# Reading the moving columns of the hidden-layer products from the last to the first

## The chip, the cores and the metric

The kernel runs on one NeuronCore of one Trainium2 chip. The metric is the device time of one execution in microseconds (us). All data are 32-bit floats; the matrix products use float32r operands, that is 32-bit words whose content was rounded for a single pass through TensorE.

## The reference

Two transformer blocks over 256 tokens of width 1024. Most of the work around this change is in three feed-forward parts:

```python
def _swiglu(x, w_gate, w_up, w_down):                 # twice, D_FF = 2816
    return (jax.nn.silu(x @ w_gate) * (x @ w_up)) @ w_down

def squared_relu_mlp(xn, w_up, w_down):               # once, D_FF_2 = 4096
    return jnp.square(jax.nn.relu(xn @ w_up)) @ w_down
...
x = _layernorm(ALPHA * x + _swiglu(x, w_gate[i], w_up[i], w_down[i]), ln_ffn_g[i], ln_ffn_b[i])
...
x = x + squared_relu_mlp(rms_norm(x, norm_mlp_g[l]), w_up[l], w_down[l])
```

The rest (multi-scale pooling, a differential attention, a mixer with two attentions and a gated recurrence) isn't touched by the change.

## The kernel before

Every operand of a large product is split in two: a rounded half (`hi`) and the rest (`lo`), and a product is hi·hi + lo·hi + hi·lo. Weights come from memory in units of 128x2048 words (1 MB), which rotate through three slots `raw`, `w_hi`, `w_lo`. For each unit SyncE issues two DMAs, ScalarE writes `w_hi` (`round_unit`, L1137), VectorE writes `w_lo = raw - w_hi` (`rest_unit`, L1149), and TensorE uses both. Semaphores `hi_done`, `lo_done` and `unit_done` tie these together; the order on each engine is written out by hand, and there are 308 / 2 = 154 units.

The activations lie in `x_both`, eight blocks of 512 words per partition: in block k the 256 tokens of `x_hi` and behind them the 256 tokens of `x_lo`. There is a second view of the same memory, `x_far`, that begins `SHIFT = 48` words later. `normed` says which stage fills and reads which: the feed-forward parts use the unshifted `x_both`, the attention, the mixer and the gates of the mixer use the shifted one.

A feed-forward part works in chunks of 256 hidden channels. One chunk of gate, and one of up, is one unit each: two PSUM banks (128 hidden channels each), eight blocks k of the contraction. `project_apart` does such a unit in two passes. In the first, `w_hi` is stationary and all 512 columns of `x_both` move, so that the bank holds in one half the product with `x_hi` and in the other that with `x_lo` (16 matmuls of 512 columns). In the second, `w_lo` is stationary and the 256 columns of `x_hi` move (16 matmuls of 256 columns), added into the first half of the bank. The function `apart` issues both. VectorE then adds the two halves of both banks with one TENSOR_REDUCE (`both_halves`, L1628), after which come the nonlinearity, a rounding into `h_hi` and `h_lo`, and the product with `w_down` (`rows`). There `h` is stationary and 512 columns of `w_hi` or `w_lo` move.

The first chunk of each part is done another way (`first_gate_up`, `in_rows`: `x` is stationary), and the last one too, by `project`: for each k three matmuls of 256 columns, `w_hi` by `x_hi`, `w_hi` by `x_lo`, `w_lo` by `x_hi`. `project` is also what the attention, the mixer and the gates use, there with the shifted view:

```python
for k in range(nk):
    c = slice(j * P, (j + 1) * P)
    last = three(o, whi[:, k, c], wlo[:, k, c], hi[:, k, :], lo[:, k, :], k == 0, k == nk - 1)
```

All matmuls go through the helper `mm`, so that the profile lists them under L506. In a name such as `bank<-x_both,w_lo` the matmul writes the bank; where `w` and `x_both` both stand, the names don't say which moves, but the column count does: 128x512 or 128x256 of `x_both,w_...` are those of `apart` and `project` with `x_both` moving; `w_...,x_both` and `w_...,arena_r` are those with the weights moving. The 128 columns of the stationary operand are loaded by an instruction of their own (LDWEIGHTS, engine PEld), which overlaps the matmul before.

One place in the kernel already reads from the last column to the first: in `v_logits` (L1757) VectorE adds a bias `table[:, slot, BACKWARDS[i]]` from SBUF.

Of the kernel before, what the change touches and what calls it, by code (L numbers as in the profile page):

```python
# [21 lines left out]
P = 128  # L22
SEQ = 256
# [154 lines left out]
def build(nc, t, out):  # L178
    with ExitStack() as ctx:
# [12 lines left out]
        x_both, x_far = (x_cells[:, at:at + KT * 2 * SEQ].rearrange("p (k t) -> p k t", k=KT) for at in (0, SHIFT))  # L192
# [72 lines left out]
        banks8 = ctx.enter_context(nc.psum_tensor("bank", [P, 8, 512], F32))  # L265
# [239 lines left out]
        def mm(*a, **k):  # L505
            return nc.tensor.matmul(*a, skip_group_check=True, **k)  # L506
# [16 lines left out]
        def apart(banks, w, cols, ks, first):  # L523

            for j, b in enumerate(banks):
                for k in ks:
                    last = mm(b[:, 0:cols], w[:, k, j * P:(j + 1) * P], x_both[:, k, 0:cols],
                              start=(first and k == 0), stop=(not first and k == KT - 1))
            return last

        def project_apart(slot, banks, narrow_first=False, between=None):

            turns = [(part(w_hi, slot, KT), 2 * SEQ), (part(w_lo, slot, KT), SEQ)]
            if narrow_first:
                turns.reverse()
            for n, (w, cols) in enumerate(turns):
                if n and between:
                    between()
                last = apart(banks, w, cols, range(KT), n == 0)
            return last  # L540

        def first_apart(eng, unit, rounds, banks):

            whi, wlo = (part(w, unit % SLOTS, KT) for w in (w_hi, w_lo))
            eng.wait_ge(hi_done, 2 * unit + 2)
            for h in range(2):
                eng.wait_ge(x_ready, 4 * rounds + 2 * h + 2)
                apart(banks, whi, 2 * SEQ, range(4 * h, 4 * h + 4), True)
            eng.wait_ge(lo_done, unit + 1)
            return apart(banks, wlo, SEQ, range(KT), False)  # L550
# [982 lines left out]
        V = nc.vector  # L1533
# [91 lines left out]

        def both_halves(o, b):

            return V.tensor_reduce(o, banks8[:, b:b + 2, :].rearrange("p a (h t) -> p a t h", h=2),  # L1628
                                   mybir.AxisListType.X, ALU.add)

        def v_ffn(eng, f):
            u0 = U_FFN[f]

            def gate_total(i, gate_unit):

                eng.wait_ge(unit_done, gate_unit + 1)
                both_halves(gate_sum, 4).then_inc(gate_read, 1)
# [7 lines left out]
            def hidden(i, up_unit, direct=None):  # L1645
                eng.wait_ge(unit_done, up_unit + 1)
                total = direct
                if direct is None:
                    both_halves(up_sum, 6).then_inc(up_read, 1)
                    eng.wait_ge(up_read, i + (f * NCH + 1))  # L1650
                    total = up_sum.rearrange("p a b -> p (a b)")
                eng.wait_ge(silu_done, i + (f * NCH + 1))
                ins = V.scalar_tensor_tensor(ffn_h, ffn_t, 0.5, total, ALU.mult, ALU.mult)
                ins.then_inc(product_done, 1)
                if direct is not None:
                    eng.wait_ge(product_done, i + (f * NCH + 1))
                    eng.sem_inc(up_read, 1)
# [38 lines left out]
        def v_mlp(eng):  # L1696
            def square(i, unit, fresh=False, final=False, b=4):
                eng.wait_ge(unit_done, unit + 1)
                if final:
                    eng.wait_ge(relu_done, 2)  # L1700
                    total, other = bank[4], ffn_e
                else:
                    both_halves(gate_sum, b).then_inc(up2_read, 1)
                    eng.wait_ge(up2_read, i + 1)
                    total = other = gate_sum.rearrange("p a b -> p (a b)")
                if not fresh:
                    eng.wait_ge(m_ready, i)
                V.scalar_tensor_tensor(ffn_h, total, 0.0, other, ALU.max, ALU.mult).then_inc(sq_done, 1)
# [467 lines left out]
```

## Time and profile before

| | |
|---|---|
| time, median of 3 runs | 950.97 us (950.43 to 951.21) |
| span of the profiled execution, first to last instruction | 949.5 us |
| granted TensorE clock over the span | 1.000 of full speed |
| PE busy | 938.3 us, 99% |
| PEld busy | 830.4 us, 87% |
| DVE busy | 668.8 us, 70% |
| ACT busy | 473.1 us, 50% |
| DMA | 185 GB/s on average |

The profiled execution spans 949.5 us between its first and last instruction, 1.5 us less than the median of the runs. A matmul's duration in the profile runs to its modelled end, while the next has already begun, so the time that a matmul costs is the distance from its start to the next one's start. It is read from the start times of merged rows: start of the next row minus start of this one, over the count.

### The profile page before, as it was taken

The page shows a single profiled execution, that of the slowest core. Times are in us where ns is not written, and L with a number is a line of the kernel's source. Part 1 is how long each engine was busy: PE and PEld are TensorE (multiplying, and loading weights), DVE is VectorE, ACT ScalarE, POOL GpSimd, SP SyncE. Part 2 cuts the span into 40 slices and gives each one's busy share as a digit, 9 for nine tenths or more (in the row PEclk, how much of TensorE's full clock was granted, in tenths as well). Part 3 has the DMA queues.
Part 4 walks back from the last instruction along what each step waited for, and adds up shares of the span by engine and source line. Part 5 has one row for each costly group of instructions (what it writes and reads, how often), then busy time and mean ns, then how long its engine had stood idle before and what let it go on. Part 6 is the DMA issues. An engine that isn't in the chain of part 4 may idle for free.

```text
span 949.5 us, 15378 instructions
## 1 busy us (share of the span) xinstructions
PE 938.3 (99%) x5895; PEld 830.4 (87%) x5895; DVE 668.8 (70%) x964; ACT 473.1 (50%) x730; POOL 34.6 (4%) x63
## 2 busy tenths in 40 slices
PE   9999999999999999999999999999999999999997
PEld 7988888888898988888887889899999888888886
DVE  4876767676787886667668587975976676666663
ACT  4544444435666454443445566568664454434432
POOL 2010001000000001000001000000000000000000
PEclk9999999999999999999999999999999999999999
DMA  8686666539533377665653945444665546655531
GB/s 295 202 284 227 199 219 209 204 133 266 147 130 101 117 249 256 213 207 178 206 182 109 265 137 134 136 134 137 219 217 181 193 142 213 203 181 189 208 135 44
DMA packets 141648, 175.67 MB, mean 185 GB/s; under 512 B 7152, under 2 KB 119985, under 8 KB 141598
## 3 DMA queue, kind: packets, MB, share of 16 engines
q1 hardware_dynamic: 138384, 166.55, 54.5%
q0 software_dynamic: 2656, 8.31, 2.5%
q8 instruction: 34, 0.56, 0.2%
q10 hardware_dynamic: 558, 0.12, 0.1%
q14 instruction: 16, 0.13, 0.0%
HBM read 173.88 MB, written 1.09 MB: 184 GB/s over the span
## 4 chain that ended last, share of the span: by engine, by line
PE 93%; DVE 5%; issue 1%; ACT 1%; POOL 0%; DVEq 0%; POOLq 0%
PE bank L506 91%; DVE w_lo L1149 1%; PE bank L844 1%; PE bank L638 1%; DVE x_rows L1573 1%; DVE x_rows L1580 1%; DVE stats L1565 1%; ACT w_hi L1137 0%; DVE x_both L1552 0%; DVE arena L2011 0%; PE bank L650 0%; ACT arena L1310 0%; DVE arena L1824 0%; PE bank L717 0%; DVE vareps L1541 0%
## 5 line engine op out<-in xcount | busy, mean ns | idle before, releaser
L1149 DVE TENSOR_TENSOR w_lo<-raw,w_hi 128x1024 fp32r<-128x1024 f32 x308 | 362.6, 1220 | 87.3 <-ACT w_hi L1137 86.8
L506 PE MATMUL bank<-x_both,w_hi 128*128 128x256 f32 (+2 forms) x2032 | 408.3, 325 | 0.0
L506 PEld LDWEIGHTS bank<-x_both,w_hi 128*128 128x128 f32 (+1 forms) x2032 | 336.7, 188 | 37.0 <-issue 5.5
L1137 ACT ACTIVATE w_hi<-raw 128x1024 fp32r<-128x1024 f32 x308 | 307.9, 1050 | 98.1 <-PE bank L506 93.6
L506 PE MATMUL bank<-x_both,w_lo 128*128 128x256 f32 (+1 forms) x1432 | 272.4, 281 | 0.0
L506 PEld LDWEIGHTS bank<-x_both,w_lo 128*128 128x128 f32 (+1 forms) x1432 | 217.0, 190 | 2.6
L506 PE MATMUL bank<-w_hi,arena_r 128*128 128x512 f32 x672 | 189.6, 391 | 0.2 <-DVE arena_r L1712 0.2
L506 PEld LDWEIGHTS bank<-w_hi,arena_r 128*128 128x128 f32 x672 | 124.6, 188 | 25.6 <-issue 0.8
L506 PE MATMUL bank<-w_lo,arena_r 128*128 128x512 f32 x336 | 106.2, 389 | 0.0
L1628 DVE TENSOR_REDUCE arena<-bank 128x512 f32<-128x1024 f32 x52 | 63.5, 1222 | 47.9 <-PE bank L506 47.9
L506 PE MATMUL bank<-w_hi,x_both 128*128 128x512 f32 (+1 forms) x352 | 75.8, 346 | 0.6 <-ACT w_hi L1137 0.4
L506 PEld LDWEIGHTS bank<-w_lo,arena_r 128*128 128x128 f32 x336 | 63.1, 188 | 13.2
L506 PEld LDWEIGHTS bank<-w_hi,x_both 128*128 128x128 f32 x352 | 55.4, 189 | 9.9 <-issue 2.0
L1206 ACT ACTIVATE arena<-arena 128x512 f32<-128x512 f32 x20 | 12.6, 632 | 82.0 <-DVE arena L1628 82.0
L506 PE MATMUL bank<-arena 64*128 64x256 f32 (+7 forms) x346 | 49.1, 351 | 3.2 <-ACT arena L1310 2.2
L1217 ACT ACTIVATE arena_r<-arena 128x512 fp32r<-128x512 f32 x20 | 12.7, 634 | 67.3 <-PE bank L506 61.5
L506 PEld LDWEIGHTS bank<-arena 64*128 64x128 f32 (+2 forms) x346 | 33.7, 186 | 12.6 <-issue 5.9
L506 PE MATMUL bank<-w_lo,x_both 128*128 128x512 f32 (+1 forms) x176 | 41.2, 342 | 0.0
L1310 ACT ACTIVATE arena<-bank 128x512 f32<-128x512 f32 x22 | 13.1, 597 | 49.4 <-PE bank L506 49.4
L1661 DVE TENSOR_TENSOR arena_r<-arena,arena_r 128x512 fp32r<-128x512 f32 x20 | 13.8, 691 | 28.8 <-ACT arena_r L1217 28.8
L1244 ACT ACTIVATE arena_r<-arena 128x512 fp32r<-128x512 f32 x15 | 9.5, 634 | 48.7 <-PE bank L506 47.9
L506 PE MATMUL bank<-arena_r,w_hi 128*128 128x256 f32 x192 | 32.9, 276 | 0.0
(179 smaller groups left out, 604.3 us busy)
## 6 DMA issues: line engine op xcount, KB each, us to landing
raw<-w_up SPq DMA_DIRECT2D x76, 512.0 KB, 4.5
raw<-w_down SPq DMA_DIRECT2D x76, 512.0 KB, 4.2
raw<-w_in SPq DMA_DIRECT2D x60, 512.0 KB, 4.6
raw<-w_gate SPq DMA_DIRECT2D x44, 512.0 KB, 4.7
raw<-w_qkv SPq DMA_DIRECT2D x24, 512.0 KB, 4.8
raw<-w_o SPq DMA_DIRECT2D x16, 512.0 KB, 4.3
table<-bias_vectors POOLq DMA_DIRECT2D x12, 256.0 KB, 4.8
raw<-w_pa SPq DMA_DIRECT2D x4, 512.0 KB, 4.4
```

Of the source, the lines that this page charges most:

```text
L506: return nc.tensor.matmul(*a, skip_group_check=True, **k)
L638: last = nc.tensor.transpose(b[:, k * P:(k + 1) * P], src[:, i, (4 * h + k) * P:(4 * h + k + 1) * P], ident[:, :])
L844: last = nc.tensor.transpose(bank[6 + m][:, c], prob[:, m, c], ident[:, :])
L1137: nc.scalar.activation(w_hi[slot][:, c], raw[slot][:, c], ACT.Copy).then_inc(hi_done, 1)
L1149: last = nc.vector.tensor_tensor(w_lo[slot][:, c], raw[slot][:, c], w_hi[slot][:, c].bitcast(F32), ALU.subtract)
L1206: nc.scalar.activation(ffn_e.rearrange("p (a b) -> p a b", a=2), gate_sum, ACT.Tanh, scale=0.5).then_inc(tanh_done, 1)
L1217: nc.scalar.activation(h_hi[buf], hidden_rows, ACT.Copy).then_inc(h_rounded, 1)
L1244: nc.scalar.activation(h_hi[buf], hidden_rows, ACT.Copy).then_inc(m_rounded, 1)
L1310: nc.scalar.activation(dst, both, ACT.Copy).then_inc(proj_copied, 1)
L1565: ins = V.bn_stats(stats[:, i, h, :], acc[i][h])
L1628: return V.tensor_reduce(o, banks8[:, b:b + 2, :].rearrange("p a (h t) -> p a t h", h=2), mybir.AxisListType.X, ALU.add)
L1661: V.tensor_tensor(h_lo[buf], ffn_h.rearrange("p (a b) -> p a b", a=2), h_hi[buf].bitcast(F32), ALU.subtract).then_inc(h_ready, 1)
```

## The change

`apart` reads the moving columns from the last to the first (a step of -1 word), for both passes. The bank then holds the columns reversed: `x_lo` reversed in its first half, `x_hi` reversed in its second; so the second pass adds into the second half. `both_halves` reads its tokens backwards from PSUM, and what it writes is in the old order. Nothing else changes: no instruction is added, removed or moved on any engine, no wait and no buffer is different. 52 units are concerned: for each feed-forward part with a gate, the gate chunks 1 to 10 and the up chunks 1 to 9 (19, twice), and in the MLP the up chunks 1 to 14.

```diff
@@ apart @@
                 for k in ks:
-                    last = mm(b[:, 0:cols], w[:, k, j * P:(j + 1) * P], x_both[:, k, 0:cols],
+                    last = mm(b[:, 2 * SEQ - cols:], w[:, k, j * P:(j + 1) * P], x_both[:, k, cols - 1::-1],
                               start=(first and k == 0), stop=(not first and k == KT - 1))
@@ both_halves @@
-            return V.tensor_reduce(o, banks8[:, b:b + 2, :].rearrange("p a (h t) -> p a t h", h=2),
+            return V.tensor_reduce(o, banks8[:, b:b + 2, :].rearrange("p a (h t) -> p a t h", h=2)[:, :, SEQ - 1::-1, :],
                                    mybir.AxisListType.X, ALU.add)
```

## Rows read from the trace of the kernel before

**Rows 1.** The page: busy time of each engine, and the chain that ended last
```profile
PE 938.3 (99%) x5895; PEld 830.4 (87%) x5895; DVE 668.8 (70%) x964; ACT 473.1 (50%) x730; POOL 34.6 (4%) x63
PE 93%; DVE 5%; issue 1%; ACT 1%; POOL 0%; DVEq 0%; POOLq 0%
```
**Rows 2.** Groups by shape, PE and DVE: count | busy us, mean ns | idle before
```profile
L506 PE MATMUL bank<-x_both,w_lo 128*128 128x256 f32 x1424 | 270.1, 281 | 0.0
L506 PE MATMUL bank<-x_both,w_hi 128*128 128x512 f32 x832 | 197.7, 390 | 0.0
L1628 DVE TENSOR_REDUCE arena<-bank 128x512 f32<-128x1024 f32 x52 | 63.5, 1222 | 47.9 <-PE bank L506 47.9
```
**Rows 3.** Timeline of PE, one gate and one up unit: start us, us, count
```profile
119.05 3.79 PE L506 MATMUL bank<-x_both,w_hi 128*128 128x512 f32 x16
122.67 4.00 PE L506 MATMUL bank<-x_both,w_lo 128*128 128x256 f32 x32
126.50 3.82 PE L506 MATMUL bank<-x_both,w_hi 128*128 128x512 f32 x16
130.16 0.61 PE L506 MATMUL bank<-w_hi,arena_r 128*128 128x512 f32 x2
```
**Rows 4.** Timeline of PE and DVE, one MLP chunk
```profile
849.49 3.79 PE L506 MATMUL bank<-x_both,w_hi 128*128 128x512 f32 x16
...
853.12 2.08 PE L506 MATMUL bank<-x_both,w_lo 128*128 128x256 f32 x16
...
855.03 0.63 PE L506 MATMUL bank<-w_hi,arena_r 128*128 128x512 f32 x2
855.23 1.22 DVE L1628 TENSOR_REDUCE arena<-bank 128x512 f32<-128x1024 f32 x1 [1.56 <-PE bank L506]
...
857.10 2.35 DVE L1149 TENSOR_TENSOR w_lo<-raw,w_hi 128x1024 fp32r<-128x1024 f32 x2
...
860.50 0.84 PE L506 MATMUL bank<-x_both,w_hi 128*128 128x512 f32 x3
```
**Rows 5.** Timeline of PE, `project` with the shifted view (27 triples)
```profile
660.24 0.39 PE L506 MATMUL bank<-x_both,w_hi 128*128 128x256 f32 x2
660.46 0.28 PE L506 MATMUL bank<-x_both,w_lo 128*128 128x256 f32 x1
...
669.42 0.39 PE L506 MATMUL bank<-x_both,w_hi 128*128 128x256 f32 x2
```
**Rows 6.** Timeline of PE, `project` unshifted (16 triples) and what follows
```profile
926.54 0.40 PE L506 MATMUL bank<-x_both,w_hi 128*128 128x256 f32 x2
926.77 0.28 PE L506 MATMUL bank<-x_both,w_lo 128*128 128x256 f32 x1
...
932.29 0.40 PE L506 MATMUL bank<-w_hi,arena_r 128*128 128x512 f32 x1
```
**Rows 7.** Loads by tile, ns min/median/max: second pass (start), second pass (middle), first pass
```profile
L506 PEld LDWEIGHTS bank<-x_both,w_lo x2: 188/188/188, 122.4 to 122.7; 128*128 128x128 f32 x2
L506 PEld LDWEIGHTS bank<-x_both,w_lo x26: 192/192/192, 122.9 to 125.9; 128*128 128x128 f32 x26
L506 PEld LDWEIGHTS bank<-x_both,w_hi x15: 187/188/188, 119.0 to 122.2; 128*128 128x128 f32 x15
```
**Rows 8.** Loads by tile, 660.3 to 671 us, `project` with the shifted view
```profile
L506 PEld LDWEIGHTS bank<-x_both,w_hi x64: 187/188/188, 660.1 to 670.8; 128*128 128x128 f32 x64
```
**Rows 9.** Timeline of PE, `project` shifted, a unit of the attention (6 triples)
```profile
255.74 0.40 PE L506 MATMUL bank<-x_both,w_hi 128*128 128x256 f32 x2
...
257.86 0.40 PE L506 MATMUL bank<-x_both,w_hi 128*128 128x256 f32 x2
```
**Rows 10.** Groups by shape, DVE: the backward read of the table
```profile
L1757 DVE CUSTOM_DVE_ANT_0 arena<-bank,table 128x256 f32<-128x256 f32 x24 | 10.1, 420 | 0.0
...
L1757 DVE CUSTOM_DVE_ANT_0 arena<-bank,table 128x128 f32<-128x128 f32 x24 | 6.9, 288 | 5.7 <-PE bank L506 5.0 <-DVE arena L1814 0.7
```
**Rows 11.** Timeline of PE, transposes of 128 plain float32 columns
```profile
763.70 1.03 PE L638 MATMUL bank<-ident,arena 128*128 128x128 f32 x8
764.57 0.61 PE L506 MATMUL bank<-ident 128*128 128x128 f32 x4
```

## Prediction

> **What bounds the kernel.** I read the page first: TensorE is busy 99% of the span and carries 93% of the chain that ended last, with VectorE at 5% [rows 1]. Nothing else needs to be known to say that only a change of the matmuls' own pace, or a stall of TensorE, can move the time. The groups by shape then give the sizes: 832 matmuls of 512 columns in first passes, and 16 for each of 52 units, so 832 again, in second passes (they are part of the 1424 with 256 columns), and 52 reductions of 1222 ns [rows 2].
>
> The pace comes from the timeline. First pass: (122.67 - 119.05) / 16 = 226.3 ns, and in the MLP (853.12 - 849.49) / 16 = 226.9 ns; about 0.443 ns per column, the same in both [rows 3, 4]. Second pass: (126.50 - 122.67) / 32 = 119.7 ns, and in the MLP (855.03 - 853.12) / 16 = 119.4 ns; 0.467 ns per column [rows 3, 4]. All 52 units together: 832 x 226.5 + 832 x 119.6 = 188.4 + 99.5 = 288 us, 30% of the span. The reader should see that the second pass is slower per column than the first, by 119.6 - 226.5 / 2 = 6.4 ns a matmul.
>
> That difference isn't a property of 256-column matmuls. `project` with the shifted view does 81 of them in 669.42 - 660.24 = 9.18 us, 113.3 ns each [rows 5]; the same function unshifted does 48 in 932.29 - 926.54 = 5.75 us, 119.8 ns each [rows 6]. Both keep TensorE full, both read the same words at the same step; only the address of the moving operand differs, by 48 words. So where the moving read begins relative to the stationary one costs 6.5 ns. The loads show the same: 188 ns where the pace is 113.3 [rows 8], 192 ns in the middle of an unshifted second pass, but 188 for its first two, and 188 in the first pass, which is unshifted too [rows 7]. The loss thus appears only when one load follows another every 256 columns, so that a load's last reads fall together with the first reads of the matmul that it serves. A 512-column matmul leaves the load 113 ns of room, and loses nothing. I read this as a collision in SBUF between the end of the stationary read and the start of the moving read; the addresses of the first start at multiples of 128 words, those of the second at multiples of 512.
>
> **The change, part by part.**
>
> *Instructions.* None is added, removed or moved; the cost can only be in the pace of what is there.
>
> *First pass, 832 matmuls.* The amount read is the same. If a step of -1 streams like +1, the cost is 0: the pace stays 226.5 ns, since the load has room. What would the step itself cost? No matmul of the trace reads its moving operand backwards. The nearest row is on another engine: VectorE's sum with the backward table takes 288 ns for 128 columns and 420 ns for 256, so (420 - 288) / 128 = 1.03 ns a column [rows 10]. The forward reduction takes at most 1222 / 1024 = 1.19 ns per element read, its fixed part included [rows 2], so the backward read has no penalty there. Lower bound 0, upper bound by the row in which a TensorE column costs most, the plain float32 transposes: (764.57 - 763.70) / 8 = 109 ns for 128, 0.85 ns a column against 0.443, a factor of 1.9 or about 2 [rows 11]. I take 0, because the only backward row says 0.
>
> The Trainium skill ("Vector Engine (DVE) Microarchitecture Reference", Measured stream behaviour on trn2) says that a VectorE port streams at full rate only in runs of two adjacent words that begin on an 8-byte boundary, and gives 1.30 ns a column for pairs that begin on an odd word against 1.054. A backward read begins on an odd word (511 or 255), so the rule, if it went by the first word read, would speak against the change. By that ratio, 1.23, an estimate from the page, the two passes would cost 832 x 0.23 x (226.5 + 113.3) ns = 65 us more, where the row gives 0. The row of the backward table, which also begins on odd words (127 and 255), doesn't bear that reading of the rule out on VectorE.
>
> *Second pass, 832 matmuls.* The moving read now begins at word 255 of its block instead of word 0, and ends at word 0. If the collision is between the load's end and the matmul's start, it depends on which words these are. Fastest end: the pace of the shifted view, 113.3 ns, a gain of 119.6 - 113.3 = 6.3 ns x 832 = 5.2 us. Between: one unit of the attention runs shifted at (257.86 - 255.74) / 18 = 117.8 ns [rows 9], which would give 1.8 x 832 = 1.5 us. Slow end without a new mechanism: another 6.5 ns, that is 126. I take the fast end. The stationary read ends at one edge of its 128 words; if it ran upwards its end would be an edge 127 against a moving start at 0, and the collision would have to be between different words; if it runs downwards it ends at word 0, where the moving read begins, and both meet. 
>
> *The reduction, 52 times.* It reads 1024 words of PSUM in pairs that lie 256 words apart, and goes through the tokens downwards instead of upwards. No row shows a backward PSUM read; the table row bounds it from below at 0, and twice its length, +1222 ns, is the bound from above. I take 0. In the MLP it is also covered: it ends at 856.45, and TensorE asks for that bank again at 860.50, 4.05 us later; the split of weights that it would delay, 857.10 to 859.45, is for the unit that starts after the next one, at about 866 [rows 4]. So even doubled it would cost nothing; without that cover it would be 52 x 1.22 = 63 us.
>
> *Sum.* 0 - 5.2 + 0 = -5.2 us. On the profiled execution 949.5 becomes 944.3; the runs lie 1.5 us above their span, so 950.97 becomes 945.7. Everything is gained on the path: TensorE is never idle there, its groups show 0.0 us of idle time before them [rows 2], and VectorE at 70% and ScalarE at 50% [rows 1] have room to follow a pace that is 1 to 2% quicker.
>
> **Rivals.**
>
> *No change.* The collision stays: the other edge of the moving block meets the load just as the first did (a load that ends at its word 127 would meet a start at 255, the same place in a period of 128 words), and the second pass remains at 119.6. For it: all block addresses are multiples of 128 words, so the mirrored start is as aligned as the old one. Time 951.0.
>
> *Slower, mildly.* Both reads now run downwards from an aligned edge at the same moment, and the moving read loses the 6.5 ns of a collision twice in 512 columns, also in the first pass, where until now it lost nothing: 832 x 13 ns = 10.8 us with the second pass as it was. Time 961.8. It decides from the moment that a first-pass matmul takes more than 226.5 + 6.3 = 232.8 ns, because then it eats the gain of the second.
>
> *Slower by much.* TensorE takes in a column in 0.443 ns, faster than any row shows for another engine; if it does so by fetching two neighbouring words at once, and does this only upwards, a column costs about twice: 832 x (226.5 + 113.3) = 283 us, less the 5.2 us at most. Time about 1230. For it: the rate in [rows 3] needs some such fetch, and no row shows it downwards on TensorE. Against it: VectorE at full rate downwards [rows 10]. The page's figure for odd words, above, would be a lighter form of the same mechanism, and shares its chance.
>
> **How the numbers follow.** Gain by a freed second pass (945.7, own range 944.8 to 949): 0.43. No change (within 0.2%, which is about what a measurement of this kernel can tell): 0.26. Mildly slower: 0.12. Much slower: 0.19. The likeliest is 945.7. A range from 944.5 to 963 holds the first three, 0.81; the much slower case is left out. A partial gain such as 117.8 ns (949.5) lies at the border and is counted half to each side. So: faster 0.42, same 0.27, slower 0.31.
>
> **What would show it.** In the timeline of the changed kernel, the second pass of a gate and an up unit should take 32 x 113.3 = 3.63 us instead of 3.83, and the loads under it 188 ns instead of 192; the first pass should still be 226.5 ns a matmul; the reduction 1222 ns. If the loads stay at 192, the collision didn't move. If first-pass matmuls are at 233 ns or more, or near 450, one of the two slower rivals is right. I'd be wrong altogether if the step of -1 changes the rate of the stream, since 30% of the span hangs on it.

## The result and the profile after

The changed kernel takes 954.75 us, the median of 5 runs (954.36 to 955.15), beside 950.65 us (950.43 to 951.21) for 5 runs of the kernel before. The ratio is 1.0042, with a 95% interval of 1.0029 to 1.0054: slower by 0.4%, about 4 us. The prediction said 945.7 us and faster. In the table further down, the 949.37 us of `second_back` are the median of 12 runs of which one took 1032.06 us at a granted clock of 0.851; without it, as in the ratio, the median is 949.30 us.

The page of the changed kernel, its span, its busy times and the chain that ended last; these answer to [rows 1]:

```profile
span 953.4 us, 15378 instructions
PE 942.2 (99%) x5895; PEld 829.4 (87%) x5895; DVE 668.6 (70%) x964; ACT 472.9 (50%) x730; POOL 35.1 (4%) x63
PE 93%; DVE 5%; issue 1%; ACT 1%; POOL 0%; DVEq 0%; POOLq 0%
```

The span grew by 953.4 - 949.5 = 3.9 us, and PE's busy time by 942.2 - 938.3 = 3.9 us. The busy time of the loads (PEld) fell by 1.0 us, that of the other engines changed by at most 0.5, the chain reads as before, and the granted clock is 0.999 against 1.000. So no wait has come in and nothing has been reordered: the matmuls themselves take longer. The groups by shape of the changed kernel say which ones; they answer to [rows 2]:

```profile
L506 PE MATMUL bank<-x_both,w_lo 128*128 128x256 f32 x1424 | 269.1, 280 | 0.0
L506 PE MATMUL bank<-x_both,w_hi 128*128 128x512 f32 x832 | 202.8, 398 | 0.0
L1628 DVE TENSOR_REDUCE arena<-bank 128x512 f32<-128x1024 f32 x52 | 63.5, 1221 | 50.9 <-PE bank L506 50.9
```

The 832 matmuls of the first passes went from 390 to 398 ns, the mean of the 256-column group fell by 1 ns, and the backward reduction is unchanged at 1221 ns. The paces stand in the timeline of PE of the changed kernel (start us, us, count), the same gate and up unit as in [rows 3]:

```profile
119.69 3.90 PE L506 MATMUL bank<-x_both,w_hi 128*128 128x512 f32 x16
123.43 3.95 PE L506 MATMUL bank<-x_both,w_lo 128*128 128x256 f32 x32
127.21 3.90 PE L506 MATMUL bank<-x_both,w_hi 128*128 128x512 f32 x16
130.95 0.63 PE L506 MATMUL bank<-w_hi,arena_r 128*128 128x512 f32 x2
```

The 32 matmuls in a row are two second passes: the kernel issues the up unit of a feed-forward part with a gate in the other order, its 256-column pass first (`narrow_first` in `project_apart`), so that the row at 127.21 is the up unit's pass of 512 columns.

First pass: (123.43 - 119.69) / 16 = 233.8 ns a matmul, before 226.3. Second pass: (127.21 - 123.43) / 32 = 118.1 ns, before 119.7. The loads under that second pass, by tile (ns min/median/max), answer to the second line of [rows 7]:

```profile
L506 PEld LDWEIGHTS bank<-x_both,w_lo x31: 187/188/189, 123.4 to 127.0; 128*128 128x128 f32 x31
```

They are back at 188 ns, from 192, and yet the pace is 118.1 and not 113.3 ns. That already speaks against the prediction's reading, in which the long load and the slow pace were one collision.

To see where the whole time went, I added up, for each kind of matmul, the distances from each one's start to the next matmul's start. These sums are worked out from all 5895 start times of each trace; since PE is never long without work, they make up the span but for its ends. In us (worked out before rounding, so that differences can be off by 0.1 from those of the rows):

| kernel | first passes, 832 of 512 columns | `w_lo` by `x_both`, 1432 of 256 | `w_hi` by `x_both`, 1200 of 256 | all other matmuls | time, median | ratio to before, 95% |
|---|---|---|---|---|---|---|
| before | 189.2 | 172.8 | 140.2 | 440.2 | 950.65 | |
| changed | 194.3 | 171.7 | 140.3 | 440.1 | 954.75 | 1.0042 [1.0029, 1.0054] |
| first_back | 194.4 | 173.0 | 140.0 | 439.7 | 956.02 | 1.0052 [1.0039, 1.0065] |
| second_back | 188.8 | 171.9 | 140.6 | 439.4 | 949.37 | 0.9978 [0.9970, 0.9987] |
| second_both | 188.8 | 172.1 | 140.0 | 439.1 | 949.05 | 0.9977 [0.9968, 0.9986] |
| before_shift | 194.1 | 167.9 | 139.5 | 440.0 | 950.98 | 0.9998 [0.9990, 1.0007] |
| after_shift | 194.2 | 171.3 | 139.7 | 440.0 | 954.08 | 1.0031 [1.0019, 1.0043] |
| rest_shift | 189.5 | 171.2 | 140.1 | 439.5 | 949.32 | 0.9981 [0.9972, 0.9990] |
| rest_16 | 189.2 | 171.6 | 140.0 | 439.9 | 948.84 | 0.9976 [0.9966, 0.9987] |
| both_16 | 191.2 | 168.4 | 139.4 | 440.4 | 947.84 | 0.9966 [0.9952, 0.9979] |

For the change: first passes +5.1 us, the `w_lo` matmuls -1.1 us, the rest within 0.1. Together +4.0, the span's 3.9. Each kernel's ratio is against runs of the kernel before on the same chip (medians of 950.65 to 951.23 us). The other rows are the experiments below; their names are used there.

### The profile page after: what moved, and what is told of

The parts are those of the page before. It is cut to its first block, busy times and chain, and to the rows that moved or that the text cites. A ratio compares the mean times of both kernels' runs of the same rounds, so it can differ in the third digit from the quotient of the medians.

```text
span 953.4 us, 15378 instructions
## 1 busy us (share of the span) xinstructions
PE 942.2 (99%) x5895; PEld 829.4 (87%) x5895; DVE 668.6 (70%) x964; ACT 472.9 (50%) x730; POOL 35.1 (4%) x63
## 4 chain that ended last, share of the span: by engine, by line
PE 93%; DVE 5%; issue 1%; ACT 1%; POOL 0%; DVEq 0%; POOLq 0%
PE bank L506 91%; DVE w_lo L1149 1%; PE bank L844 1%; PE bank L638 1%; DVE x_rows L1573 1%; DVE x_rows L1580 1%; DVE stats L1565 1%; ACT w_hi L1137 0%; DVE x_both L1552 0%; DVE arena L2011 0%; PE bank L650 0%; ACT arena L1310 0%; DVE arena L1824 0%; PE bank L717 0%; DVE vareps L1541 0%
## 5 line engine op out<-in xcount | busy, mean ns | idle before, releaser
L506 PE MATMUL bank<-x_both,w_hi 128*128 128x256 f32 (+2 forms) x2032 | 413.5, 328 | 0.0
L1628 DVE TENSOR_REDUCE arena<-bank 128x512 f32<-128x1024 f32 x52 | 63.5, 1221 | 50.9 <-PE bank L506 50.9
```

## The experiments

### The two passes apart

`first_back` turns only the first pass, `second_back` only the second. Of `first_back` the edit in `apart` is this; `second_back` has the two branches the other way round, and both read backwards in the reduction as the change does. Each of them then adds columns of different tokens to one another; the amount of work is that of the change.

```diff
-                    last = mm(b[:, 0:cols], w[:, k, j * P:(j + 1) * P], x_both[:, k, 0:cols],
+                    move = x_both[:, k, cols - 1::-1] if cols == 2 * SEQ else x_both[:, k, 0:cols]
+                    last = mm(b[:, 2 * SEQ - cols:], w[:, k, j * P:(j + 1) * P], move,
```

first_back:

> Only the first pass (512 columns, hi weights) reads backwards; the second pass reads forwards but still adds into the upper half of the bank, so its columns are added in the wrong order (the amount of work is unchanged). If the cost of the change sits in the first pass alone, every one of its 832 matmuls takes 233.3 instead of 226.7 ns: +5.1 to 5.5 us, about 956.0 us. Rival, that the two passes influence each other through the order in which they follow: less than +4 us. Second pass: 119.7 ns, as before, if its gain in the changed kernel came from its own direction; about 118.3 if it came from what precedes it.

second_back:

> Only the second pass (256 columns, lo weights) reads backwards; the first reads forwards into the bank, so the halves are summed in mixed order (wrong sums, same work). Theory that start positions matter: first pass back at 226.7 ns, second pass at about 118.3 ns as in the changed kernel, so about 1.2 us less than before, 949.4 us. Rival, that a step of -1 is what costs: second pass slower than 119.7, time above 951.

The timeline of PE of `first_back`, and then of `second_back`, at the same place in the program:

```profile
119.50 3.90 PE L506 MATMUL bank<-x_both,w_hi 128*128 128x512 f32 x16
123.23 4.00 PE L506 MATMUL bank<-x_both,w_lo 128*128 128x256 f32 x32
127.07 3.90 PE L506 MATMUL bank<-x_both,w_hi 128*128 128x512 f32 x16
```

```profile
118.39 3.79 PE L506 MATMUL bank<-x_both,w_hi 128*128 128x512 f32 x16
122.02 3.95 PE L506 MATMUL bank<-x_both,w_lo 128*128 128x256 f32 x32
125.81 3.79 PE L506 MATMUL bank<-x_both,w_hi 128*128 128x512 f32 x16
```

`first_back`: 233.1 ns in the first pass and (127.07 - 123.23) / 32 = 120.0 in the second. `second_back`: 226.9 and (125.81 - 122.02) / 32 = 118.4. So each pass carries its own share: the backward first pass costs 5.2 us in the sums, the backward second pass gives back 0.9 us, and 0.4 us more comes from first passes that run at 226.9 (in the kernel before they are at 226.3 and at 228.8 in turn, [rows 3]). Another 0.8 us of `second_back`, and 1.1 us of `second_both` below, lies in the other matmuls, which the edits don't touch; the sums are of one execution each, and what made that part isn't shown. The loss is in the first pass, to which the prediction had given a cost of zero.

### Another place for the moving read

If the start address is what counts, the unshifted activations can be moved instead. `before_shift` is the kernel before, with both views at 48; `after_shift` is the changed kernel with the same edit.

```diff
-... for at in (0, SHIFT))
+... for at in (SHIFT, SHIFT))
```

before_shift:

> The kernel before, but all stages use the view that begins 48 words later (forward reading). Theory of a collision at the place where the moving read begins: second pass at 113.3 instead of 119.7 ns, 832 x 6.3 = 5.3 us less, and the unshifted project units gain 144 x 6.5 = 0.9 us: about 944.6 us. Rival, that the 48 words act only where the three products of project alternate: no change, 950.7 us.

after_shift:

> The changed kernel with the same shift by 48 words everywhere. Theory that the backward read is slow only because it begins at the last word of a block, the same place modulo 128 words at which the stationary read begins: first pass back at 226.7 and second at 113.3 ns, about 944.6 us, the same as forwards with the shift. Rival, that the step of -1 itself costs 16 cycles a matmul: first pass stays at 233.3 ns, about 950 us or more.

The timeline of PE of `before_shift`:

```profile
118.53 3.89 PE L506 MATMUL bank<-x_both,w_hi 128*128 128x512 f32 x16
122.26 3.80 PE L506 MATMUL bank<-x_both,w_lo 128*128 128x256 f32 x32
125.90 3.89 PE L506 MATMUL bank<-x_both,w_hi 128*128 128x512 f32 x16
```

Forward, 48 words further, the second pass does run at (125.90 - 122.26) / 32 = 113.8 ns, and the first at 233.1 ns, in nothing but a forward read. The sums say -4.9 us and +4.9 us, and the time is that of before (0.9998), not the 944.6 us expected: the rival's time, but not by the rival's reason, since the second pass did gain. In `after_shift` both stay where the backward read has put them: 233.1 and 117.8 ns, by (122.74 - 119.01) / 16 and (126.51 - 122.74) / 32. So the backward read doesn't answer to the shift, and 512-column matmuls do lose 6.7 ns at an offset that 256-column ones like.

### The matmuls alone

Four kernels hold nothing of the reference but matmuls: float32r words of value one in SBUF, eight blocks of 512 moving columns and of two times 128 stationary ones as in `x_both` and a unit, 16 to 32 matmuls for each configuration (in `micro4` twice a single one), straight after one another. Each of the four was executed once, at a granted clock of 1.00 in all the rows used here. The stationary tensor alternates, so that each configuration is a row of its own in the timeline, and the pace is once more start of the next row minus start of this one, over the count. That average holds the few matmuls in which the pace settles too. Each configuration also has another one just before it; that this matters comes out at the end, in `micro4`.

`micro1` sweeps the direction and the offset of the moving read:

```python
at = k * 512 + shift
a = moving[:, at:at + width]
if back:
    a = moving[:, at:at + width][:, ::-1]
s = src[:, k * 256 + (i // 8 % 2) * P + w_shift:][:, 0:P]
```

> Only matmuls, 24 to a configuration, all of the reference left out: 512 or 256 moving columns, forwards or backwards, the moving operand shifted by 0 to 127 words and then the stationary one by 16, 48 or 64. Theory of places: the pace depends on shift and direction together. 512 forwards 226.7 at all shifts; 512 backwards 233.3 at shift 0 and 226.7 at 48; 256 forwards 120 at 0 and 113.3 at 48; 256 backwards about 118 at 0. Over the shifts each slow case should fill a stretch as wide as one piece of memory that can serve one reader at a time, and come back with a period. Rival, that the step costs by itself: 512 backwards 233.3 at every shift.

The timeline of PE of `micro1`. In this order: 512 forward at offset 0 and (next row) 4; 512 backward at offset 0 and 4; 256 forward at 0 and 4, and at 16, 32 and 48; then 512 forward at offset 0 with the stationary read moved by 16 and (next row) by 48 words.

```profile
20.00 5.60 PE L66 MATMUL bank<-moving,w_even 128*128 128x512 f32 x24
25.44 5.72 PE L66 MATMUL bank<-moving,w_odd 128*128 128x512 f32 x24
...
86.55 5.76 PE L66 MATMUL bank<-moving,w_even 128*128 128x512 f32 x24
92.15 5.76 PE L66 MATMUL bank<-moving,w_odd 128*128 128x512 f32 x24
...
154.00 3.03 PE L66 MATMUL bank<-moving,w_even 128*128 128x256 f32 x24
156.87 3.02 PE L66 MATMUL bank<-moving,w_odd 128*128 128x256 f32 x24
...
162.53 2.89 PE L66 MATMUL bank<-moving,w_odd 128*128 128x256 f32 x24
165.25 3.01 PE L66 MATMUL bank<-moving,w_even 128*128 128x256 f32 x24
168.09 2.89 PE L66 MATMUL bank<-moving,w_odd 128*128 128x256 f32 x24
...
222.10 5.75 PE L66 MATMUL bank<-moving,w_even 128*128 128x512 f32 x24
227.69 5.66 PE L66 MATMUL bank<-moving,w_odd 128*128 128x512 f32 x24
```

512 columns: (25.44 - 20.00) / 24 = 226.7 ns forward, (92.15 - 86.55) / 24 = 233.3 backward. 256 columns at 16: (165.25 - 162.53) / 24 = 113.3 forward. The whole sweep, worked out the same way from unrounded start times, so that a value can differ by some tenths from the rounded rows:

| ns a matmul, by offset in words | 0 | 4 | 8 | 16 | 32 | 48 | 64 | 80 | 96 | 112 | 120 | 127 |
|---|---|---|---|---|---|---|---|---|---|---|---|---|
| 512 forward | 226.7 | 231.5 | 233.5 | 228.9 | 232.1 | 233.3 | 227.5 | 229.6 | 232.8 | 233.5 | 233.2 | 230.3 |
| 512 backward | 233.3 | 233.3 | 233.4 | 233.4 | 236.6 | 233.2 | 233.5 | 233.5 | 233.5 | 233.2 | 233.5 | 239.8 |
| 256 forward | 119.6 | 119.1 | 116.7 | 113.5 | 118.5 | 113.8 | 119.2 | 118.0 | 118.5 | 117.8 | 118.2 | 117.0 |
| 256 backward | 118.1 | 120.0 | 118.0 | 119.9 | 119.8 | 118.0 | 118.3 | 119.7 | 119.8 | 118.0 | 117.7 | 120.3 |

For 512 columns forward, 64 to 112 read like 0 to 48, within 1 ns: a period of 64 words. For 256 columns 64 reads like 0, but 80 and 112 don't read like 16 and 48. With the moving read at 0 and the stationary one moved by 16, 48 or 64 words instead, 512 backward stays at 233.2 to 233.3. But 512 forward doesn't stay at 226.7: it takes 233.0, 229.2 and 227.1 ns, and 256 forward 114.3, 113.3 and 119.9. So the good pace of a forward read hangs on where the stationary read lies as well: moving that one alone by 16 words costs (227.69 - 222.10) / 24 - 226.7 = 6.2 ns, about what the backward read costs.

So a forward read has better and worse offsets, and 226.7 at offset 0 is the best of them for 512 columns; a backward read has no good one among these twelve, nor among the three places of the stationary read. A theory of the start address, mine or the rival's, would have one.

`micro2` takes what would collide away: the same matmuls with 96, 64 and 32 stationary columns, so that the load reads down to a quarter of the words. It also has moving reads with a step of 2.

```python
a = moving[:, at:at + width * step:step]
...
s = src[:, k * 256 + (i // 8 % 2) * P:][:, 0:m]      # m = 128, 96, 64, 32
```

> Only matmuls again, 24 to a configuration, the reference left out: stationary operands of 128, 96, 64 and 32 columns under the same moving reads, then 128 and 384 moving columns, odd starts and steps of 2. Theory that the 16 cycles are a collision of the backward moving read with the stationary read that runs beside it: they shrink with the stationary columns, 512 backwards about 233.3, 231.7, 230.0, 228.3 ns for 128, 96, 64, 32, and don't depend on the moving columns (384 backwards 6.7 ns over 384 forwards). Rival, that a step of -1 costs the moving read itself: 233.3 whatever the stationary operand, and the loss goes with the moving columns (256 backwards half of 512). Third, a fixed cost of starting a backward read: 6.7 ns at every size of both.

512 columns backward at offset 0 took 233.2, 236.4, 233.3 and 233.2 ns with 128, 96, 64 and 32 stationary columns; forward 226.7, 230.2, 230.5 and 231.5. 256 columns forward took 119.2, 116.2, 114.1 and 113.8, and backward 118.3, 119.8, 117.6 and 117.8. The backward 512-column pace doesn't fall with the stationary read. The gap to the forward one does, from 6.5 to 1.7 ns, but because the forward read gets slower, not because the backward one gets faster. Of the 256-column reads the forward one got faster here; `micro3` below has 117.9 ns for that same read over 32 stationary columns, so that isn't a property of the narrow stationary operand alone. Nor is the loss a fixed fee: with 128 stationary columns, over the last twelve matmuls of each row, 384 columns took 173.3 ns forward and 177.8 backward, and 128 columns 111.7 either way. The steps of 2, from the timeline of PE of `micro2` (128 stationary columns with step 2, then step -2; 32 with step 2):

```profile
202.46 5.60 PE L72 MATMUL bank<-moving,w_even 128*128 128x256 f32 x24
207.88 5.78 PE L72 MATMUL bank<-moving,w_odd 128*128 128x256 f32 x24
213.48 5.66 PE L72 MATMUL bank<-moving,w_even 128*32 128x256 f32 x24
```

(207.88 - 202.46) / 24 = 225.8 ns for 256 columns: a step of 2 costs as much as 512 neighbouring words, with step -2 233.3, as much as 512 words backwards. That is what one would see if words came in pairs at least, as the much-slower rival said; but then they come downwards as well, since a step of -1 costs 3%, not 100%.

`micro3` asks how far apart the pieces must be that are read in the wrong order. It reads 512 columns in groups of g words: either the words within each group downwards and the groups upwards ("words"), or the groups downwards and the words within upwards ("groups"). A second sweep changes the width, with 32 stationary columns.

```python
a = a.rearrange("p (a b) -> p a b", b=g)
a = a[:, :, ::-1] if way == "words" else a[:, ::-1, :]
```

> Only matmuls, 32 to a configuration, the reference left out. 512 moving columns of one block, reversed in part: either the words inside groups of 2 to 256 run down while the groups run up, or the groups run down while their words run up. Then 64 to 512 columns, up and down, under a stationary operand of 32 columns. Theory that a backward read pays a fixed part at its start: one step back in a group costs nothing, groups of any size with words downwards stay near 226.7, and down minus up is 4 to 7 ns at every width. Rival, that the cost goes with the words read downwards (through some piece of memory of a certain size): down minus up grows from 1 ns at 64 columns to 6.7 at 512, and the cost changes at one group size.

The timeline of PE of `micro3` (the table below it is from unrounded starts again): up, down; words of 4, groups of 4, words of 8, groups of 8, words of 16, groups of 16; groups of 32, words of 64, groups of 64, words of 128.

```profile
20.55 7.42 PE L68 MATMUL bank<-moving,w_even 128*128 128x512 f32 x32
27.80 7.63 PE L68 MATMUL bank<-moving,w_odd 128*128 128x512 f32 x32
...
50.01 7.43 PE L68 MATMUL bank<-moving,w_even 128*128 128x512 f32 x32
57.28 7.63 PE L68 MATMUL bank<-moving,w_odd 128*128 128x512 f32 x32
64.75 7.62 PE L68 MATMUL bank<-moving,w_even 128*128 128x512 f32 x32
72.21 7.63 PE L68 MATMUL bank<-moving,w_odd 128*128 128x512 f32 x32
79.67 8.70 PE L68 MATMUL bank<-moving,w_even 128*128 128x512 f32 x32
88.20 7.64 PE L68 MATMUL bank<-moving,w_odd 128*128 128x512 f32 x32
...
103.14 7.61 PE L68 MATMUL bank<-moving,w_odd 128*128 128x512 f32 x32
110.59 7.63 PE L68 MATMUL bank<-moving,w_even 128*128 128x512 f32 x32
118.06 7.43 PE L68 MATMUL bank<-moving,w_odd 128*128 128x512 f32 x32
125.33 7.63 PE L68 MATMUL bank<-moving,w_even 128*128 128x512 f32 x32
```

| ns a matmul of 512 columns, by g | 2 | 4 | 8 | 16 | 32 | 64 | 128 | 256 |
|---|---|---|---|---|---|---|---|---|
| words down, groups up | 227.2 | 227.2 | 233.1 | 266.4 | 233.3 | 233.3 | 233.4 | 233.4 |
| groups down, words up | 233.4 | 233.4 | 233.4 | 233.7 | 232.6 | 227.2 | 227.2 | 227.2 |

Up to four words read in the wrong order cost nothing once the pace has settled (226.7 ns over the last twelve; the 227.2 hold two slower matmuls at the start), as long as the fours go upwards, and neither do stretches of 64 or more in the wrong order. Everything else costs 6 to 7 ns, and 16 words turned round cost 40. In these runs the loss follows the order in which pieces of at least 4 words are read inside a stretch of 64 words. It is not a fee for a start or a turn, since a read of 256 turned pairs pays nothing and one of two turned halves of 256 words pays all of it.

The Trainium skill ("Advanced Engine Details and Errata", Memory Cachelines) says that SBUF has lines of 16 bytes, which is 4 words, and that accesses which stay on the same line run at full rate. The free turn of 4 words, 227.2 ns in the table above, agrees with that; that turned stretches of 64 words are free while turned ones of 8 to 32 aren't is not in that rule, nor is the cost of fours read upwards but taken in falling order, 233.4 ns.

The width sweep, up and down: 117.9 and 117.8 ns at 256 columns, 146.3 and 146.7 at 320, 173.4 and 175.6 at 384, 202.2 and 204.5 at 448, 231.3 and 233.2 at 512. Below 384 columns the two directions differ by at most 0.4 ns in this sweep; at 256 columns `micro2` had 113.8 and 117.8 ns for the same two reads, behind other ones.

### The second pass by other means

`second_both` asks whether the gain of the backward second pass needs a backward write. The first pass is forward; the second reads and writes its bank backwards, so every sum is the reference's:

```diff
+                    out_, move = b[:, 0:cols], x_both[:, k, 0:cols]
+                    if cols == SEQ:
+                        out_, move = b[:, cols - 1::-1], x_both[:, k, cols - 1::-1]
...
```

> The kernel before, but the second pass alone reads backwards and also writes its bank backwards, so that the halves stay in order and the sums are right; the reduction reads forwards. If only the moving read's direction counts: second pass at 118.2 ns as in the changed kernel, first at 226.7, about 949.4 us. Rival, that a backward write to PSUM costs: second pass above 119.7, time above 951.

226.9 and (125.68 - 121.90) / 32 = 118.1 ns, 949.05 us: like `second_back`. Writing PSUM backwards costs nothing that shows.

`rest_shift` and `rest_16` keep both reads forward at offset 0 and move the stationary side: `w_lo` of the hidden-layer units lies 48 or 16 words further in a wider tile. The three tiles are wider by 64 words each, so that what is laid out behind them may lie further on too, by a multiple of 64 words.

```diff
+        w_lo_cells = [sb(f"w_lo{s}", [P, UW + 64], F32R) for s in range(SLOTS)]
...
+        w_lo_far = [v[:, SHIFT:SHIFT + UW] for v in w_lo_cells]      # 16 in rest_16
...
-            turns = [(part(w_hi, slot, KT), 2 * SEQ), (part(w_lo, slot, KT), SEQ)]
+            turns = [(part(w_hi, slot, KT), 2 * SEQ), (part(w_lo_far, slot, KT), SEQ)]
```

rest_shift:

> The kernel before, forwards, with w_lo of the gate, up and MLP-up units written and read 48 words further on, so that the second pass has the offset at which 256 columns took 113.3 ns in the first microbenchmark, while the first pass keeps the offset 0 at which 512 columns take 226.7. Theory that the pace is set by the distance of the two read addresses modulo 64 words: second pass 113.3 instead of 119.7, 832 x 6.3 = 5.3 us, and the row products and projects that use this w_lo (128 matmuls) 0.9 us more: about 944.7 us. Rival, that the gain of the second pass is given back in the first, as it was when both were shifted: 950.7 us.

rest_16:

> As the version with w_lo of the hidden units 48 words further on, but 16 words. If the pace is set by the distance of the two addresses modulo 64 words, 16 and 48 are not the same; in the first microbenchmark both gave 113.3 ns at 256 columns. If the second pass reaches 113.3: about 945 us. If it stays at the 117.6 ns at which the 48-word version settled: about 949.3 us.

Second passes at (125.31 - 121.55) / 32 = 117.5 and (126.40 - 122.63) / 32 = 117.8 ns, first passes at 226.9: 949.32 and 948.84 us. The 113.3 ns of the matmuls alone, which `micro1` gave for the stationary shifts of 16 and 48, didn't come, with one exception inside `rest_shift` itself: worked out from single starts, the 33 passes that stand right behind a pass of 512 columns settle at 118 ns, and the 3 that have four transposes in between (`between` in `project_apart`) at 113; in `rest_16` it is 2 of those 3. The same 256-column matmul, at the same offsets, thus has more than one pace, and something else decides. `micro4` asks whether it is the pass before: 16 matmuls of 512 columns, then 32 of 256, at varied offsets; at its end reads up and down in turn.

> Only matmuls, the reference left out, in the order in which the kernel has them: 16 of 512 columns at offset 0 and then 32 of 256 with the stationary or the moving operand at another offset; then matmuls of 512 and of 256 columns read upwards and downwards in turn. Theory that the pace of a pass depends on the state in which the pass before leaves the two reads: 256 columns at offset 48 settle at 117.6 ns behind 512 columns at offset 0, as in the kernel, and at 113.3 behind 512 at offset 48. Rival, that something else of the kernel (other engines' accesses) holds it at 117.6: 113.3 in both. In the mixed passes, if the loss lies in the hand-over from one matmul to the next, up-down and down-up differ from one another; if it lies inside a downward read, the matmul read downwards takes 233.3 and the one read upwards 226.7.

The timeline of PE of `micro4`: 512 at offset 48, 256 at offset 48; 512 at 16, 256 at 16; 512 at 0, 256 at 48, 512 at 0, 256 at 16, and the next row.

```profile
73.06 3.89 PE L78 MATMUL bank<-moving,w_even 128*128 128x512 f32 x16
76.78 3.93 PE L78 MATMUL bank<-moving,w_odd 128*128 128x256 f32 x32
80.55 3.84 PE L78 MATMUL bank<-moving,w_even 128*128 128x512 f32 x16
84.23 3.79 PE L78 MATMUL bank<-moving,w_odd 128*128 128x256 f32 x32
87.86 3.81 PE L78 MATMUL bank<-moving,w_even 128*128 128x512 f32 x16
91.51 3.93 PE L78 MATMUL bank<-moving,w_odd 128*128 128x256 f32 x32
95.28 3.83 PE L78 MATMUL bank<-moving,w_even 128*128 128x512 f32 x16
98.95 3.93 PE L78 MATMUL bank<-moving,w_odd 128*128 128x256 f32 x32
102.72 3.82 PE L78 MATMUL bank<-moving,w_even 128*128 128x512 f32 x16
```

The same 32 matmuls at offset 16, on the same words: (87.86 - 84.23) / 32 = 113.4 ns behind 512-column ones at offset 16, and (102.72 - 98.95) / 32 = 117.8 behind 512-column ones at offset 0. The pace is kept for the whole pass. Of what I varied, only the pass before differs between the two (the bank written is another one too), so it is the pass before that sets the pace; the three passes behind transposes in `rest_shift` say the same inside the kernel.

Which pass before gives which pace, these runs don't show. At offset 48 the expectation failed: behind 512 columns at 48, 256 at 48 took (80.55 - 76.78) / 32 = 117.8 ns, no less than behind 512 at 0, while the same sequence in `before_shift` took 113.8. There, too, 2 of the 3 passes behind transposes settle at 118 ns, the other way round than in `rest_shift`. And behind 512 columns at 0, none of the seven places of the stationary read gave 113.3: they took 116.6 to 120.1 ns.

With reads up and down in turn, 512 columns took 230.0 ns on average, in the middle between 226.7 and 233.3. From single starts it is 228 ns behind each upward start and 232 behind each downward one. That fits a loss that stays with the matmuls that read downwards, but a loss in the hand-over from one direction to the other would alternate too.

### What the runs point to

At offset 16 a pass of 512 columns takes between 226.7 and 233.3 ns a matmul, and in `micro4` the pass of 256 columns behind it took 113.4. `both_16` is the kernel before, both passes forward, with the feed-forward view 16 words further; one number changes.

```diff
-... for at in (0, SHIFT))
+... for at in (16, SHIFT))
```

> The kernel before, forwards, with the feed-forward view of x_both 16 words further on (the attention and mixer keep their 48). By the microbenchmarks, 512 columns at offset 16 take 229 ns and the 256 behind them 113.3, where behind 512 at offset 0 they stay at 117.6: first pass +2.5 x 832 = 2.1 us, second pass -6.3 x 832 = -5.2 us, the last chunks' project units (144 matmuls) -1.0 us, the output projection of the mixer, whose stationary operand moves with the view, up to +0.8 us: about 947.5 us. Rival, that the first pass gives back what the second gains, as with 48 words everywhere: 950.9 us.

The timeline of PE of `both_16`:

```profile
118.47 3.84 PE L506 MATMUL bank<-x_both,w_hi 128*128 128x512 f32 x16
122.16 3.79 PE L506 MATMUL bank<-x_both,w_lo 128*128 128x256 f32 x32
125.78 3.82 PE L506 MATMUL bank<-x_both,w_hi 128*128 128x512 f32 x16
```

(122.16 - 118.47) / 16 = 230.6 and (125.78 - 122.16) / 32 = 113.1 ns. In the sums the first passes cost 1.9 us more, the 256-column matmuls 4.5 + 0.8 us less. At 947.84 us (947.78 to 948.18), ratio 0.9966 [0.9952, 0.9979], it beats both kernels: 3.3 us under the one before, and about 7 under the changed one.

## Why the prediction was wrong

**What bounds the kernel: right.** TensorE's pace alone moved the time. The 3.9 us of the span are the 3.9 us of PE.

**First pass, cost 0: wrong, and this step decides the sign.** It is +5.1 us, that is 6.1 ns on each of 832. The 0 rested on one backward row, of another engine [rows 10], and on "the amount read is the same", together with the reading that a 512-column matmul leaves the load room and so loses nothing. That reading fails even forwards: at offset 48 the first pass takes 233.1 ns (`before_shift`). `first_back` shows the loss when only this pass is turned, `micro1` shows 226.7 against 233.3 ns with nothing else in the kernel, and `micro3` what it hangs on there: the order of the pieces inside 64 words. The prediction gave "slower" a chance of 0.31.

**Second pass, -5.2 us: right in sign, a fifth in size.** It gained 1.1 us, at 118.1 ns and not 113.3. The premise was that the address where the moving read begins costs 6.5 ns, and that a start at word 255 instead of 0 frees it. `before_shift` bears out the first half for a forward read (113.8 ns, -4.9 us), but the backward read never comes to 113.3, at any of twelve offsets. The load's 192 ns, which I had taken for the mark of the collision, went to 188 without the pace. And one row on record said as much: the attention runs with the shifted view at 117.8 ns [rows 9], so that one offset already had two paces. I named that value, and took the end of the range instead.

**A collision with the stationary read: nothing shows it for the backward read.** With 32 stationary columns instead of 128 the 512 backward columns still take 233.2 ns, and 233.2 to 233.3 wherever the stationary read was put. For forward reads the prediction was right that the two reads bear on one another: moving the stationary read alone took 512 columns from 226.7 to 233.0 ns, and 256 from 119.6 to 113.3, each in one row of `micro1`. What passes between the two isn't shown, so that it stays open whether the backward read is slow by itself, or is one that never gets into the good relation.

**Reduction, cost 0: right.** 1221 ns against 1222 ns, and no wait behind it. The timeline of the changed kernel, one MLP chunk, answers to [rows 4]:

```profile
858.69 1.22 DVE L1628 TENSOR_REDUCE arena<-bank 128x512 f32<-128x1024 f32 x1 [1.66 <-PE bank L506]
860.55 2.35 DVE L1149 TENSOR_TENSOR w_lo<-raw,w_hi 128x1024 fp32r<-128x1024 f32 x2
```

**The rivals.** "No change" is out by the interval. "Much slower" is out: whatever makes a step of 2 cost double works downwards as well. The reading of the Trainium skill's odd-word rule ("Vector Engine (DVE) Microarchitecture Reference", Measured stream behaviour on trn2) that went with it gave 65 us; the change cost 4, so a factor of 1.23 didn't show here on TensorE. "Slower, mildly" had the sign, the place (the first pass) and even the point at which it decides, 232.8 ns, with 233.3 measured. Its price was twice too high, since it counted two losses of 6.5 ns where there is one of 6.7, and its mechanism, an aligned edge where both reads meet, is refuted as far as the first pass goes: by `after_shift`, in which the moving read lies 48 words off the edge and still takes 233.1 ns, and with it `micro2`.

**Open.** What the pieces of 4 to 32 words are physically, why turned groups of 16 cost 40 ns, and how the pass before can set the pace of the next, in which cases it does, and why `micro4` and `before_shift` differ at offset 48. The 0.7 and 0.5 us by which the 1200 forward matmuls of `w_hi` gained in `before_shift` and `after_shift` weren't looked into.

## What to carry to other kernels

Where TensorE is the bound, the order and the offset of the moving read are part of its pace, at the level of 3 to 6% of a matmul. Read it forward, and choose its offset by measuring the passes in their real sequence, since the pass before counts, and the best offset for 512 columns (0) isn't that for 256 (16 or 48 here). A kernel of nothing but matmuls isn't that sequence: `rest_shift` and `rest_16` missed what `micro1` promised. A row of another engine is weak evidence for a rate of this one: a few dozen matmuls in a kernel of their own would have settled the term that decided this prediction. And where one offset shows two paces in the trace, neither is a property of the offset.

## What the runs showed of the hardware

- 512 moving float32r columns backwards: 233.3 ns against 226.7 forwards at offset 0. Turned in groups of 16 words: 266.4 ns. Turned in 2 or 4 words, or in stretches of 64 and more: 227.2 ns.
- Among the twelve offsets of `micro1` that of a forward moving read is worth up to 6.8 ns at 512 columns, with a period of 64 words, and up to 6.1 ns at 256, with other good places. The place of the stationary read counts too: moved alone by 16 words, 512 forward took 233.0 ns instead of 226.7.
- One 256-column pass on the same words ran at 113.4 or at 117.8 ns, by the offset of the 512-column pass before it (0 or 16 words); at offset 48 `micro4` and `before_shift` disagree, 117.8 and 113.8 ns.
- A step of 2 words doubles the time of a column: 256 columns took 225.8 ns, 512 neighbouring ones 226.7.
- Reading PSUM backwards (VectorE, 1221 ns against 1222) and writing it backwards (TensorE, 118.1 against 118.4 ns) costs nothing that can be seen.
